# A residual stage that also prepares the next one, and filler products between the rotary stage and the compression

## The chip, the cores and the metric

The kernel runs on one core of a Trainium2 chip. The metric is the device time of one execution, in microseconds (us); lower is better.

## The reference

Two blocks of two layers each work on 512 tokens of width 1024; the second block has 256 context tokens beside them. Around each product stands a norm and a residual:

```python
def rms_norm(x, g):
    xf = x.astype(jnp.float32)
    y = xf * lax.rsqrt(jnp.mean(xf * xf, axis=-1, keepdims=True) + RMS_EPS)
    return (y * g.astype(jnp.float32)).astype(x.dtype)

def hybrid_layer(...):                       # first block, 2 layers
    hn = rms_norm(x, norm_g[0])
    ... = split_columns(hn @ w_in)           # queries, keys, values, gates
    kc = compress_blocks(k_c, cmp_pe[0], cmp_w1[0], cmp_w2[0])   # gelu(blocks @ w1) @ w2
    ks = partial_rope(k_s, positions)
    ...
    x = x + rms_norm(mixed, norm_g[1])
    hf = rms_norm(x, norm_g[2])
    ff = jnp.square(jax.nn.relu(hf @ w_ff1)) @ w_ff2
    return x + rms_norm(ff, norm_g[3])
```

The second block first computes `modulate(rms_norm_2(x, g), shift, scale)` over all 768 tokens and multiplies it by the latent attention's down projections; its second layer does the same ahead of a gated linear attention, whose first product is the small gate product. All is in float32; products that need the accuracy are made of three products of split operands (high and low parts).

## The kernel before

Features lie on the partitions: `x` is a tile of 128 partitions x 8 feature tiles (`KT`) x 768 tokens (512 and 256 of context). The program is a row of stages, each an `nc.Block()`, in which every engine has its own list of instructions; a stage begins when every engine has finished the one before. The two layers of the first block are one hardware loop (`nc.Fori(0, DEPTH)`).

Names that the change touches:

- `Norm`: ScalarE squares a feature tile (L237) into one of two buffers, TensorE adds it into PSUM with a product by a matrix of ones (L262); a square waits until the sum two tiles back is made. Then the root (L246, ScalarE), a turn to columns (L303, TensorE), the reciprocal and the diagonals (L316, L319, VectorE), and the spread back over the partitions (L309, TensorE). `keep_busy` issues products of constants that nothing reads (L205).
- `Normed`: VectorE scales (L355), ScalarE rounds to the high part (L368), VectorE subtracts for the low part (L346, L348); `first_tiles` multiplies feature tile by feature tile as the low parts come.
- `Residual`: VectorE scales `y` (L393); VectorE adds even tiles to `x` and GpSimd the odd ones (both L387).
- Weights come in units of 1 MB through two buffers `w_raw`; `load_unit` issues them on SyncE's queue, `split_hi` (ScalarE, L146) or `split_first` (VectorE, L411) rounds a unit, `split_lo` (VectorE, L152) subtracts.
- `sem_scope`: at its end, in a stage of its own, SyncE clears every semaphore made in it, one after the other (L2592). The layer loop's body is one scope, so this is done once in a layer, ahead of the branch (L2546).
- `stage_residual` holds nothing but a norm's spread and the residual. The stage behind it (`stage_qkv` at the head of a layer, `stage_modulation` and `stage_norm_dense` "down" at the head of the second block, `stage_norm_dense` "gate1" in its second layer) loads its small tables and two weight units, squares and sums `x`, and takes the root, then multiplies.
- `stage_rope`: TensorE permutes, VectorE and GpSimd rotate. `stage_compress`: VectorE adds positions to blocks (L604), TensorE multiplies them (L616, 64 instructions that are all queued behind each other).

Of the kernel before, what the change touches and what calls it, by code (L numbers as in the profile page):

```python
# [26 lines left out]
P = 128  # L27
# [180 lines left out]
class Norm:  # L208
# [10 lines left out]
    def __init__(self, k, name, src, kt, tok, bank, it=0, sems=None):  # L219
# [3 lines left out]
        self.name = name  # L223
# [20 lines left out]
    def act_root(self, act):  # L244
        act.wait_ge(self.summed, self.kt * (self.it + 1))
        act.activation(self.k.root[:, 0:self.tok], self.sums[0:1, :], ACT.Sqrt,  # L246
                       bias=self.k.c["eps"][0:1, 0:1]).then_inc(self.root, 1)
# [25 lines left out]
    def dve_gather(self, dve, t):  # L273
        k, tok = self.k, self.tok
        if t == 0:
            return
        acc = k.acc[:, 0:tok]
        dve.wait_ge(self.squared, t + 1)
        if t >= 2:
            dve.wait_ge(self.gathered, t - 1)  # L280
        dve.tensor_tensor(acc, k.sqt[:, 0, 0:tok] if t == 1 else acc, k.sqt[:, t % 2, 0:tok],
                          ALU.add).then_inc(self.gathered, 1)

# [148 lines left out]
def stage_qkv(nc, k, b, stream, first_unit):  # L432

    norm = Norm(k, "n1", k.x, KT, SEQ, 5)
# [4 lines left out]
    g_loaded = k.sem("g_loaded")  # L439

    with nc.Block() as block:
        @block.sync
        def _(sp):
            sp.dma_start(b.g, b.g_src).then_inc(g_loaded, 16)
            for n in range(n0, n0 + UNITS_QKV):
                load_unit(sp, k, n, stream(n))

        @block.tensor
        def _(pe):
            norm.pe_all(pe)  # L450
# [26 lines left out]
        @block.vector  # L477
        def _(dve):
            split_first(dve, k, n0)
            norm.dve_all(dve)  # L480
            dve.wait_ge(g_loaded, 16)
            normed.dve(dve)
            for u in range(2, UNITS_QKV):
                split_lo(dve, k, n0 + u)

        @block.scalar
        def _(act):
            norm.act_all(act)
# [39 lines left out]
def stage_rope(nc, k, b):  # L528
# [7 lines left out]
    with nc.Block() as block:  # L536
# [50 lines left out]
def stage_compress(nc, k, b):  # L587
# [8 lines left out]
    with nc.Block() as block:  # L596
# [13 lines left out]
        def _(pe):  # L610
# [16 lines left out]

            first_layer(0)
# [854 lines left out]
def stage_residual(nc, k, name, y, tok, post, y_norm=None):  # L1483

    norm = y_norm or Norm(k, f"{name}_p", y, KT, tok, 5)
    res = Residual(k, f"{name}_r", norm, k.x, post)
    with nc.Block() as block:  # L1487
        @block.tensor
        def _(pe):
            if y_norm is None:  # L1490
                norm.pe_all(pe)
            else:
                norm.pe_spread(pe)

        @block.scalar
        def _(act):
            if y_norm is None:
                norm.act_all(act)
            else:
                norm.act_root(act)  # L1500
# [11 lines left out]
def stage_rope_tables(nc, k, b, positions, inv_freq, inputs):  # L1512
# [8 lines left out]
    with nc.Block() as block:  # L1521
        @block.sync
        def _(sp):
            sp.dma_start(b.pos_i, positions.partition_broadcast(P)).then_inc(loaded, 16)
            sp.dma_start(b.inv, inv_freq).then_inc(loaded, 16)
            for dst, src in inputs:
                sp.dma_start(dst, src).then_inc(inputs_loaded, 16)
            sp.wait_ge(inputs_loaded, 16 * len(inputs))

        @block.vector  # L1530
        def _(dve):
# [23 lines left out]
            dve.sem_inc(sined, 1)  # L1555

# [8 lines left out]

# [9 lines left out]
def stage_modulation(nc, k, b, a, stream):  # L1575

    loaded, biased, scales = k.sem("mod_loaded"), k.sem("mod_biased"), k.sem("mod_scales")
    with nc.Block() as block:  # L1578
        @block.sync
        def _(sp):  # L1580
            for dst, src in ((b.ada_b, a["ada_b"]), (b.g, a["norm_g2"]), (b.axial, a["axial"]), (b.g_q, a["g_q"]),
                             (b.g_kv, a["g_kv"]), (b.g_o, a["g_o"])):
                sp.dma_start(dst, src).then_inc(loaded, 16)
            load_unit(sp, k, 0, stream(0))
            load_unit(sp, k, 1, stream(1))

        @block.vector
        def _(dve):
            dve.wait_ge(loaded, 96)
            dve.tensor_tensor(b.mod, b.mod, b.ada_b.unsqueeze(3).to_broadcast([P, ADA_TURNS, KT, 2]),  # L1590
                              ALU.add).then_inc(biased, 1)
            dve.wait_ge(biased, 1)
            for l in range(DEPTH):
                for j, (m, plus) in enumerate(((1, 1.0), (2, 0.0), (4, 1.0), (5, 0.0))):
                    g = b.g[:, l, j, :].unsqueeze(2).to_broadcast([P, KT, 2])
                    dve.scalar_tensor_tensor(b.sc[:, 4 * l + j, :, :], b.mod[:, 6 * l + m, :, :], plus, g, ALU.add,
                                             ALU.mult).then_inc(scales, 1)
            dve.wait_ge(scales, 4 * DEPTH)
# [12 lines left out]
def stage_norm_dense(nc, k, name, stream, n0, n_units, width, cols, out, tok, parts, after=2):  # L1611

    norm = Norm(k, f"{name}_n", k.x, KT, tok, 5)
# [3 lines left out]
    with nc.Block() as block:  # L1617
        @block.sync
        def _(sp):
            for n in range(n0 + 2, n0 + n_units + after):  # L1620
                load_unit(sp, k, n, stream(n))

        @block.tensor
        def _(pe):
            norm.pe_all(pe)
# [20 lines left out]
        def _(act):  # L1646
            norm.act_all(act)
# [721 lines left out]
def second_block(nc, k, a):  # L2369
# [3 lines left out]
    b = Bag()  # L2373
    stream = lambda n: a["stream2"][n]
    k.hhi, k.hlo = at("h_hi_2", [P, KT, TOK], F32R, 60), at("h_lo_2", [P, KT, TOK], F32R, 84)
    b.axial = at("axial", [P, TOK], F32, 108)
    b.mod = k.mod.rearrange("p (l t v) -> p l t v", t=KT, v=2)
    b.sc = at("norm_scales", [P, 4 * DEPTH, KT, 2], F32, 112.75)
    b.g_q, b.g_kv, b.g_o = at("g_q", [P, 3], F32, 113.25), at("g_kv", [P, 2], F32, 113.3125), at("g_o", [P, 2], F32, 113.375)
    b.st = at("mla_stat", [P, 8, 3], F32, 113.5)  # L2380
    b.ada_b, b.g = at("ada_b", [P, ADA_TURNS, KT], F32, 117), at("norm_g2", [P, DEPTH, 4, KT], F32, 118)
# [14 lines left out]
    rings(k, "second", 175)  # L2396
    mla_norm, mlp_norm = Norm(k, "mla_norm", y, KT, TOK, 1), Norm(k, "mlp0_norm", y, KT, TOK, 5)
    stage_modulation(nc, k, b, a, stream)
    n = 0

    with k.sem_scope():
        n = stage_norm_dense(nc, k, "down", stream, n, U_DOWN, UNIT, 256, down, TOK, parts_of(b, 0, 0, TOK, 0), 1)
# [6 lines left out]
    with k.sem_scope():  # L2409
        n = stage_mlp(nc, k, "mlp0", stream, n, y, hid_hi, hid_lo, TOK, parts_of(b, 0, 1, TOK), parts_of(b, 0, 2, TOK, 3), UNITS_2,  # L2410
                      mlp_norm, mla_norm)
        stage_residual(nc, k, "mlp0r", y, TOK, parts_of(b, 0, 3, TOK), mlp_norm)
# [13 lines left out]
                         parts_of(b, 1, 0, TOK, 0))  # L2426
# [16 lines left out]
def second_arrays(g, a):  # L2443
# [32 lines left out]
    a["stream2"] = np.concatenate(out)  # L2476
    assert a["stream2"].shape == (UNITS_2, P, UNIT)
# [10 lines left out]
def rings(k, sec, kb):  # L2488

    k.whi = k.at(f"w_hi_{sec}", [P, 2, UNIT], F32R, kb)  # L2490
    k.wlo = k.at(f"w_lo_{sec}", [P, 2, UNIT], F32R, kb + 16)


def first_block(nc, k, a):
# [6 lines left out]
    b.g, b.inv = at("norm_g1", [P, 4, KT], F32, 96), at("rope_inv", [P, 1], F32, 96.25)  # L2501
    b.pos_i = at("positions_i", [P, SEQ], I32, 97)
    stage_rope_tables(nc, k, b, a["positions"], a["inv_freq"],
                      [(k.x[:, :, 0:SEQ], a["x"]), (k.x[:, :, SEQ:TOK], a["ctx"]), (k.consts, a["consts"]), (k.cv, a["cvec"])])
# [41 lines left out]
    with nc.Fori(0, DEPTH) as layer, k.sem_scope(*k.w_loaded, k.w_hi, k.w_lo):  # L2546
        stream = lambda n: a["stream1"][layer, n]
        ada.layer, ada.src = layer, lambda n: a["ada_w"][layer, n]
        b.g_src = a["norm_g"][layer]
# [4 lines left out]
        n = stage_qkv(nc, k, b, stream, 0)  # L2554
# [7 lines left out]
        wo_norm, ff_norm = Norm(k, "wo_norm", y, KT, SEQ, 4), Norm(k, "ff_norm", y, KT, SEQ, 5)  # L2562
# [4 lines left out]
        stage_residual(nc, k, "ffr", y, SEQ, [(0, SEQ, b.g[:, 3, :])], ff_norm)  # L2567


def build(nc, a):  # L2570
    with ExitStack() as es:
# [9 lines left out]
        def sem_scope(*more):  # L2581
# [3 lines left out]
            with ExitStack() as stack:  # L2585
                k.scope = (stack, [])
                yield
                with nc.Block() as block:
                    @block.sync
                    def _(sp):  # L2590
                        for s in [*k.scope[1], *more]:
                            sp.sem_clear(s)  # L2592
                k.scope = outer

        k.sem, k.sem_scope = sem, sem_scope
# [8 lines left out]
        k.at = at  # L2604
# [11 lines left out]
        first_block(nc, k, a)  # L2616
        second_block(nc, k, a)
# [45 lines left out]
def host_arrays(i):  # L2663
# [8 lines left out]
    a["norm_g"] = np.ascontiguousarray(g["norm_g"].reshape(DEPTH, 4, KT, P).transpose(0, 3, 1, 2))  # L2672
# [3 lines left out]
    a["stream1"] = np.stack([stream_1(*(g[n][l] for n in ("w_in", "w_nsa_o", "w_sb_o", "w_out", "w_ff1", "w_ff2")))  # L2676
# [17 lines left out]
```

## Time and profile before

| | |
|---|---|
| time, median of 3 runs | 3806.79 us (3804.06 to 3808.51) |
| the profiled execution | 3811.21 us, of which the span from first to last instruction is 3809.4 us |
| TensorE products | 3497.2 us busy, 92% of the span |
| VectorE, ScalarE, GpSimd | 51%, 36%, 15% of the span |
| granted TensorE clock, mean | 0.961 of full |

The rows below are from that one profiled execution. A timeline row gives the start and the duration of a merged run of instructions in microseconds; in brackets stands the engine's idle time before it and what ended that. TensorE's clock is granted at one of two levels, 0.5 (1.2 GHz) and 1.0 (2.4 GHz); a value between them is a mean.

### The profile page before, as it was taken

The numbers are of one execution on the slowest core, as the hardware profiler recorded it, in microseconds if no ns is written. First come the engines' busy times: TensorE is split into PE (matmuls) and PEld (weight loads), VectorE is DVE, ScalarE is ACT, GpSimd is POOL, SyncE is SP. The second block draws the span as 40 slices with busy tenths as digits, with TensorE's granted clock in tenths as the row PEclk, the third lists the DMA queues.
The fourth block names the chain that finished last, engine by engine and source line by source line (L and its number), as shares of the span: only waits on it lengthen the run. The fifth ranks groups of instructions, "written<-read, shape, count | busy, mean of one in ns | idle before, by whom it ended". The sixth has DMA issues, their size and how long they took to land. (4 is left out here: it accounts for less than half of the span.)

```text
span 3809.4 us, 46818 instructions
## 1 busy us (share of the span) xinstructions
PE 3497.2 (92%) x17938; PEld 2880.7 (76%) x17938; DVE 1938.8 (51%) x2421; ACT 1354.8 (36%) x1976; POOL 552.5 (15%) x389
## 2 busy tenths in 40 slices
PE   8898999998889899999888989999999788889998
PEld 6675878887667687888667877888887677768886
DVE  4363347777337334777735652533334544455444
ACT  3275234443336523444323442221222423323222
POOL 0141003344024100433300110000000100010000
PEclk9999999999889899999999999999999899999999
DMA  3101224442210122444110011111111111102221
GB/s 134 69 1 56 99 100 155 154 155 76 101 58 1 66 88 100 155 162 158 67 50 23 18 36 48 56 57 65 66 59 41 44 35 44 44 33 89 96 91 66
DMA packets 58346, 287.18 MB, mean 75 GB/s; under 512 B 9824, under 2 KB 11104, under 8 KB 30944
## 3 DMA queue, kind: packets, MB, share of 16 engines
q1 hardware_dynamic: 58208, 285.34, 21.4%
q8 instruction: 87, 1.43, 0.2%
q14 instruction: 51, 0.42, 0.0%
HBM read 283.21 MB, written 2.10 MB: 75 GB/s over the span
## 5 line engine op out<-in xcount | busy, mean ns | idle before, releaser
L163 PE MATMUL ps<-h_hi,w_hi_rest 128*128 128x512 f32 (+1 forms) x1072 | 388.1, 362 | 27.4 <-DVE w_lo_rest L152 16.1
L164 PE MATMUL ps<-h_lo,w_hi_rest 128*128 128x512 f32 (+1 forms) x1072 | 366.9, 357 | 0.0
L1302 POOL TENSOR_TENSOR ada_context<-ada_context,ada_scaled 128x768 f32<-128x768 f32 x112 | 287.5, 2567 | 455.2 <-ACT ada_scaled L1384 450.1
L166 PE MATMUL ps<-h_hi,w_lo_rest 128*128 128x512 f32 (+1 forms) x1072 | 324.7, 358 | 0.0
L152 DVE TENSOR_TENSOR w_lo_mix<-w_raw,w_hi_mix 128x2048 fp32r<-128x2048 f32 x96 | 221.6, 2310 | 199.6 <-ACT w_hi_mix L146 199.5
L163 PE MATMUL ps<-h_hi,w_hi_mix 128*128 128x512 f32 x768 | 299.6, 390 | 4.6 <-DVE w_lo_mix L152 2.4
L164 PE MATMUL ps<-h_lo,w_hi_mix 128*128 128x512 f32 x768 | 299.1, 390 | 0.0
L166 PE MATMUL ps<-h_hi,w_lo_mix 128*128 128x512 f32 x768 | 299.1, 389 | 0.0
L387 POOL TENSOR_TENSOR x<-x,y 128x512 f32<-128x512 f32 (+1 forms) x32 | 63.8, 1994 | 1555.7 <-DVE y L393 1555.7
L146 ACT ACTIVATE w_hi_rest<-w_raw 128x2048 fp32r<-128x2048 f32 x82 | 156.3, 1908 | 360.1 <-PE ps L166 357.2
L1466 DVE TENSOR_TENSOR y<-ps,y 128x512 f32<-128x512 f32 (+1 forms) x224 | 165.8, 751 | 218.6 <-PE ps L166 217.9
L163 PE MATMUL ps<-hid_hi,w_hi_rest 128*128 128x512 f32 (+1 forms) x768 | 273.3, 356 | 0.0
L163 PEld LDWEIGHTS ps<-h_hi,w_hi_rest 128*128 128x128 f32 x1072 | 203.5, 190 | 80.6 <-DVE h_lo L348 14.3
L164 PE MATMUL ps<-hid_lo,w_hi_rest 128*128 128x512 f32 (+1 forms) x768 | 260.7, 354 | 0.0
L1397 ACT ACTIVATE sq<-ps 128x512 f32<-128x512 f32 (+1 forms) x128 | 83.4, 651 | 473.1 <-PE ps L166 473.1
L152 DVE TENSOR_TENSOR w_lo_rest<-w_raw,w_hi_rest 128x2048 fp32r<-128x2048 f32 (+1 forms) x85 | 195.9, 2307 | 70.3 <-ACT w_hi_rest L146 70.2
L166 PE MATMUL ps<-hid_hi,w_lo_rest 128*128 128x512 f32 (+1 forms) x768 | 231.2, 355 | 0.0
L146 ACT ACTIVATE w_hi_mix<-w_raw 128x2048 fp32r<-128x2048 f32 x94 | 178.9, 1905 | 145.2 <-PE ps L166 134.1
L164 PEld LDWEIGHTS ps<-h_lo,w_hi_rest 128*128 128x128 f32 x1072 | 203.7, 190 | 29.7
L1440 DVE SCALAR_TENSOR_TENSOR ada_latent<-ada_raw,cvec,ada_latent 128x768 f32<-128x768 f32 x112 | 225.4, 2012 | 0.0
L205 PE MATMUL ps<-consts 128*128 128x128 f32 x700 | 109.4, 313 | 112.6 <-PEq L1578 25.6
L163 PE MATMUL ps<-hid_hi,w_hi_mix 128*128 128x512 f32 x512 | 205.7, 402 | 0.1
(392 smaller groups left out, 7823.2 us busy)
## 6 DMA issues: line engine op xcount, KB each, us to landing
w_raw<-in_stream SPq DMA_DIRECT2D x205, 1024.0 KB, 4.8
ada_raw<-in_ada_w SPq DMA_DIRECT2D x128, 384.0 KB, 5.0
cmp_w<-in_cmp_w SPq DMA_DIRECT2D x8, 1024.0 KB, 7.3
mla_raw<-in_stream SPq DMA_DIRECT2D x8, 512.0 KB, 3.6
x<-in_x SPq DMA_DIRECT2D x1, 2048.0 KB, 8.6
out<-x SPq DMA_DIRECT2D x1, 2048.0 KB, 7.3
x<-in_ctx SPq DMA_DIRECT2D x1, 1024.0 KB, 10.8
consts<-in_consts SPq DMA_DIRECT2D x1, 832.0 KB, 12.0
```

The lines of the kernel that those rows point to most:

```text
L146: act.activation(k.whi[:, n % 2, 0:width], k.raw[:, n % 2, 0:width], ACT.Copy).then_inc(k.w_hi, 1)
L152: dve.tensor_tensor(k.wlo[:, n % 2, 0:width], k.raw[:, n % 2, 0:width], k.whi[:, n % 2, 0:width].bitcast(F32), ALU.subtract).then_inc(k.w_ ...
L163: pe.matmul(out, whi, xhi, start=start, stop=False)
L164: pe.matmul(out, whi, xlo, start=False, stop=False)
L166: last = pe.matmul(out, wlo, xhi, start=False, stop=stop)
L205: pe.matmul(k.ps[:, bank * 512:bank * 512 + P], k.c["ones"], k.c["ident"], start=True, stop=True)
L387: e.tensor_tensor(self.x[:, t, 0:n.tok], self.x[:, t, 0:n.tok], n.src[:, t, 0:n.tok], ALU.add).then_inc(sem, 1)
L1302: pool.tensor_tensor(ada.context, ada.context, ada.scaled[:, j % 2, :], ALU.add).then_inc(m["context"], 1)
L1397: act.activation(k.sqt[:, j % 2, 0:tok], k.ps[:, base:base + tok], ACT.Relu).then_inc(s["relu"], 1)
L1440: dve.scalar_tensor_tensor(ada.latent, ada.raw[j], k.cv[:, j, 0:1], ada.latent, ALU.mult, ALU.add).then_inc(m["latent"], 1)
L1466: dve.tensor_tensor(y[:, j, 0:tok], src, y[:, j, 0:tok], ALU.add).then_inc(s["added"], 1)
```

## The change

Four things are done.

1. `stage_residual` takes the next stage's norm with it. ScalarE squares each tile of `x` as soon as the residual has added it. At the end of a layer it also rounds the next stage's first two weight units. `x`'s norm there covers all 768 tokens, in every layer: first the eight context parts (256 columns each), then the eight parts of 512 columns, with 6 filler products between. The head of the kernel does the same in the stage of the rotary tables. The stages `qkv`, `down` and `gate1` no longer have a norm of their own.
2. SyncE issues, in the layer's last residual stage, the next layer's (or the second block's) first two weight units and seven small tables, and clears the semaphores of all stages behind it. For this it clears four semaphores of the weight ring first; ScalarE and VectorE wait for that (`reset`).
3. `stage_modulation` is gone; its nine VectorE instructions stand ahead of `normed.dve` in the stage "down". The weights of both blocks are one tensor in memory.
4. 16 products of constants at the end of TensorE's list in `stage_rope`, and 3 at the head of its list in `stage_compress`.

```diff
+    def pe_context_first(self, pe):
+        for t in range(self.kt):
+            self.pe_add_cols(pe, t, t, SEQ, CTX)
+        keep_busy(pe, self.k, 6, self.free)
+        for t in range(self.kt):
+            self.pe_add_cols(pe, self.kt + t, t, 0, SEQ)
+        self.pe_spread(pe)
+    def act_context_first(self, act, before=None):
+        for t in range(self.kt):
+            self.act_square_cols(act, t, t, SEQ, CTX)
+        for t in range(self.kt):
+            if before is not None:
+                before(act, t)
+            self.act_square_cols(act, self.kt + t, t, 0, SEQ)
+        self.act_root(act)
...
 def stage_qkv
-            sp.dma_start(b.g, b.g_src).then_inc(g_loaded, 16)
-            for n in range(n0, n0 + UNITS_QKV):
+            for n in range(n0 + 2, n0 + UNITS_QKV):
                 load_unit(sp, k, n, stream(n))
+            for sem in norm.sems:
+                sp.sem_clear(sem)
...
-            norm.pe_all(pe)
...
-            split_first(dve, k, n0)
-            norm.dve_all(dve)
-            dve.wait_ge(g_loaded, 16)
+            dve.tensor_copy(b.g, b.g_next).then_inc(g_taken, 1)
+            dve.wait_ge(g_taken, 1)
             normed.dve(dve)
...
 def stage_rope
+            pe.wait_ge(half2, 1)
+            keep_busy(pe, k, 16, 0)
...
 def stage_compress
+            keep_busy(pe, k, 3, 6)
             first_layer(0)
...
 def stage_residual
+            norm.pe_spread(pe)
+            if next_unit is not None:
+                next_norm.pe_context_first(pe)
+            elif next_norm is not None:
+                next_norm.pe_all(pe)
...
+            if reset is not None:
+                act.wait_ge(reset, 1)
+            norm.act_root(act)
+            if next_unit is not None:
+                next_norm.act_context_first(act, res.wait)
+                split_hi(act, k, next_unit + 1, (k.w_lo, next_unit + 1))
+            elif next_norm is not None:
+                next_norm.act_all(act, res.wait)
...
+            if reset is not None:
+                dve.wait_ge(reset, 1)
             norm.dve_all(dve)
             res.dve(dve)
+            if next_unit is not None:
+                res.wait(dve, KT - 2)
+                res.wait(dve, KT - 1)
+                split_first(dve, k, next_unit, 1)
+            if next_norm is not None:
+                next_norm.dve_all(dve)
+            if next_unit is not None:
+                split_lo(dve, k, next_unit + 1)
...
 def stage_rope_tables
+            for n in range(2):
+                load_unit(sp, k, n, stream(n))
             sp.wait_ge(inputs_loaded, 16 * len(inputs))
+        @block.tensor
+        def _(pe):
+            norm.pe_context_first(pe)
...
+            split_first(dve, k, 0)
+            norm.dve_all(dve)
...
             act.wait_ge(silu, 1)
-
+            norm.act_table(act)
+            norm.act_context_first(act)
...
 def stage_norm_dense
-            norm.pe_all(pe)
...
-            split_first(dve, k, n0, min(n_units, 2), width)
-            norm.dve_all(dve)
+            if before is not None:
+                before(dve)
+            if split < min(n_units, 2):
+                split_first(dve, k, n0 + split, min(n_units, 2) - split, width)
             normed.dve(dve)
...
 def first_block
+        finished = [sem for sem in k.scope[1] if sem not in ff_norm.sems]
+        reset = k.sem("ffr_reset")
+        def prefetch(sp):
+            for sem in (*k.w_loaded, k.w_hi, k.w_lo):
+                sp.sem_clear(sem)
+            sp.sem_inc(reset, 1)
+            for i in range(2):
+                load_unit(sp, k, i, a["stream"][(layer + 1) * UNITS_1 + i])
...
+            for dst, src in loads:
+                sp.dma_start(dst, src).then_inc(small_loaded, 16)
+            k.clear(sp, finished)
+            sp.wait_ge(small_loaded, 16 * len(loads))
+            sp.sem_clear(small_loaded)
```

## Rows read from the trace of the kernel before

**Rows 1.** The page, part 1: busy us (share of the span) and instructions
```profile
PE 3497.2 (92%) x17938; PEld 2880.7 (76%) x17938; DVE 1938.8 (51%) x2421; ACT 1354.8 (36%) x1976; POOL 552.5 (15%) x389
```

**Rows 2.** Timeline, end of layer 0 (start, duration, engine, line, operation, count, idle before)
```profile
936.07 0.68 ACT L246 ACTIVATE acc<-ps,consts 1x512 f32<-1x512 f32 x1 [2.21 <-PEq L1272]
939.99 1.41 DVE L393 SCALAR_TENSOR_TENSOR y<-y,norm_g,ps 128x512 f32<-128x512 f32 x2 [0.67 <-PE ps L309]
947.23 1.64 POOL L387 TENSOR_TENSOR x<-x,y 128x512 f32<-128x512 f32 x1 [0.27 <-DVE y L393]
```

**Rows 3.** Line L2592, clears, 949 to 958 us; then 2959 to 2961 us
```profile
L2592 SPq EVENT_SEMAPHORE_RANGE_CLEAR  x134: 25/30/49, 949.2 to 957.2; - x134
...
L2592 SPq EVENT_SEMAPHORE_RANGE_CLEAR  x23: 25/25/30, 2959.4 to 2960.6; - x23
```

**Rows 4.** Line L2546, the layer loop's branch (duration ns min/median/max, starts)
```profile
L2546 PEldq COMPARE_BRANCH  x2: 83/1728/3372, 957.7 to 1907.9; - x2
```

**Rows 5.** Timeline, layer 1's first norm
```profile
966.64 0.63 ACT L237 ACTIVATE sq<-x 128x512 f32<-128x512 f32 x1 [0.60 <-PE ps L262]
970.33 0.63 ACT L237 ACTIVATE sq<-x 128x512 f32<-128x512 f32 x1 [0.36 <-PE ps L262]
971.83 4.49 DVE L152 TENSOR_TENSOR w_lo_qkv<-w_raw,w_hi_qkv 128x2048 fp32r<-128x2048 f32 x2
971.98 1.05 PE L205 MATMUL ps<-consts 128*128 128x128 f32 x8
976.24 0.18 DVE L316 RECIPROCAL norm_stat<-ps 128x4 f32<-128x4 f32 x1
978.90 1.41 DVE L355 SCALAR_TENSOR_TENSOR sq<-x,norm_g,ps 128x512 f32<-128x512 f32 x2 [1.58 <-PE ps L309]
```

**Rows 6.** Timeline, start of the kernel
```profile
18.92 0.63 ACT L237 ACTIVATE sq<-x 128x512 f32<-128x512 f32 x1
29.28 0.68 ACT L246 ACTIVATE acc<-ps,consts 1x512 f32<-1x512 f32 x1 [1.22 <-PE ps L262]
33.05 1.41 DVE L355 SCALAR_TENSOR_TENSOR sq<-x,norm_g,ps 128x512 f32<-128x512 f32 x2 [0.67 <-PE ps L309]
```

**Rows 7.** Timeline, layer 1 to the second block
```profile
1897.47 1.64 POOL L387 TENSOR_TENSOR x<-x,y 128x512 f32<-128x512 f32 x1 [0.27 <-DVE y L393]
1907.92 0.35 SPq L1583 DMA_DIRECT2D ada_b<-in_ada_b  x1
1914.45 0.77 DVE L1596 SCALAR_TENSOR_TENSOR norm_scales<-mod,norm_g 128x16 f32<-128x16 f32 x8
1935.02 2.19 DVE L355 SCALAR_TENSOR_TENSOR sq<-x,norm_scales,ps 128x512 f32<-128x512 f32 x4 [0.72 <-PE ps L309]
```

**Rows 8.** Timeline, second residual to the gate product
```profile
2956.61 2.45 POOL L387 TENSOR_TENSOR x<-x,y 128x768 f32<-128x768 f32 x1 [0.50 <-DVE y L393]
2961.69 1.23 DVE L152 TENSOR_TENSOR w_lo_rest<-w_raw,w_hi_rest 128x1024 fp32r<-128x1024 f32 x1
2979.87 2.19 DVE L355 SCALAR_TENSOR_TENSOR sq<-x,norm_scales,ps 128x512 f32<-128x512 f32 x4 [0.72 <-PE ps L309]
```

**Rows 9.** Timeline, the MLP stage that already has residual and norm in one block
```profile
2379.78 3.59 POOL L387 TENSOR_TENSOR x<-x,y 128x768 f32<-128x768 f32 x1 [0.49 <-DVE y L393]
2390.59 2.19 DVE L355 SCALAR_TENSOR_TENSOR sq<-x,norm_scales,ps 128x512 f32<-128x512 f32 x4 [0.72 <-PE ps L309]
```

**Rows 10.** Timeline, rotary stage and compression of layer 0
```profile
152.21 0.42 PE L557 MATMUL ps<-consts,gate_t 24*128 24x24 f32 x4
159.59 16.04 PE L616 MATMUL ps<-cmp_w,blk 128*31 128x256 f32 x64 [6.96 <-DVE blk L604]
```

**Rows 11.** Windows there and in layer 1 (us, busy time and count of each engine, clock, DMA share, GB/s)
```profile
156.00:157.00 1.00, 0.00 (x0) 0.00 (x0) 0.97 (x2) 0.00 (x0) 0.57 (x1) 0.96 1.02 426
163.00:164.00 1.00, 1.00 (x4) 0.45 (x3) 0.00 (x0) 0.00 (x0) 0.00 (x0) 0.62 0.00 0
...
1106.00:1110.00 4.00, 3.81 (x11) 1.71 (x12) 1.57 (x4) 0.81 (x1) 0.00 (x0) 0.59 0.01 6
```

More of the change, by code:

```diff
@@ L244, in act_root @@
     def act_root(self, act):
-        act.wait_ge(self.summed, self.kt * (self.it + 1))
+        act.wait_ge(self.summed, self.adds * (self.it + 1))
         act.activation(self.k.root[:, 0:self.tok], self.sums[0:1, :], ACT.Sqrt,
@@ L282, in dve_gather, with act_square_cols, pe_add_cols @@
                           ALU.add).then_inc(self.gathered, 1)
+    def act_square_cols(self, act, i, t, c0, w):
+        k = self.k
+        if i >= 2:
+            act.wait_ge(self.summed, i - 1)
+        act.activation(k.sqt[:, i % 2, c0:c0 + w], self.src[:, t, c0:c0 + w], ACT.Square,
+                       scale=float((self.kt * P) ** -0.5)).then_inc(self.squared, 1)
+    def pe_add_cols(self, pe, i, t, c0, w):
+        k = self.k
+        pe.wait_ge(self.squared, i + 1)
+        pe.matmul(self.sums[:, c0:c0 + w], k.c["ones"], k.sqt[:, i % 2, c0:c0 + w],
+                  start=t == 0, stop=t == self.kt - 1).then_inc(self.summed, 1)
+    def act_context_first(self, act, before=None):
[13 more added lines that the diff above has]
+        self.pe_spread(pe)
     def pe_sum(self, pe):
@@ L1509, in _, with stage_rope_tables @@
             res.pool(pool)
-def stage_rope_tables(nc, k, b, positions, inv_freq, inputs):
+def stage_rope_tables(nc, k, b, positions, inv_freq, inputs, norm, stream):
     loaded, chain, sined = k.sem("rt_loaded"), k.sem("rt_chain"), k.sem("rt_sin")
@@ L1572, with modulation @@
 MLA_SCALE = float(192 ** -0.5)
[L1575 to L1598, printed above, removed]
+def modulation(dve, k, b):
+    biased, scales = k.sem("mod_biased"), k.sem("mod_scales")
+    dve.tensor_tensor(b.mod, b.mod, b.ada_b.unsqueeze(3).to_broadcast([P, ADA_TURNS, KT, 2]),
+                      ALU.add).then_inc(biased, 1)
+    dve.wait_ge(biased, 1)
+    for l in range(DEPTH):
+        for j, (m, plus) in enumerate(((1, 1.0), (2, 0.0), (4, 1.0), (5, 0.0))):
+            g = b.g[:, l, j, :].unsqueeze(2).to_broadcast([P, KT, 2])
+            dve.scalar_tensor_tensor(b.sc[:, 4 * l + j, :, :], b.mod[:, 6 * l + m, :, :], plus, g, ALU.add,
+                                     ALU.mult).then_inc(scales, 1)
+    dve.wait_ge(scales, 4 * DEPTH)
 def parts_of(b, layer, norm, tok, shift=None):
@@ L1608, in parts_of, with stage_norm_dense @@
     return out
-def stage_norm_dense(nc, k, name, stream, n0, n_units, width, cols, out, tok, parts, after=2):
-    norm = Norm(k, f"{name}_n", k.x, KT, tok, 5)
+def stage_norm_dense(nc, k, name, stream, n0, n_units, width, cols, out, tok, parts, norm, split=0, after=2, before=None):
     normed = Normed(k, f"{name}_h", norm, k.hhi, k.hlo, parts)
@@ L1621, in _ @@
                 load_unit(sp, k, n, stream(n))
+            for sem in norm.sems:
+                sp.sem_clear(sem)
         @block.tensor
         def _(pe):
-            norm.pe_all(pe)
             unit_ready(pe, k, n0)
@@ L2394, in second_block @@
     hid_hi, hid_lo = at("hid_hi2", [P, 4, TOK], F32R, 127), at("hid_lo2", [P, 4, TOK], F32R, 139)
-    rings(k, "second", 175)
-    mla_norm, mlp_norm = Norm(k, "mla_norm", y, KT, TOK, 1), Norm(k, "mlp0_norm", y, KT, TOK, 5)
-    stage_modulation(nc, k, b, a, stream)
+    rings(k, "qkv", 175)
+    mla_norm, mlp_norm = Norm(k, "mla_norm", y, KT, TOK, 1), Norm(k, "mlp0_norm", y, KT, TOK, 1)
+    gate_norm = Norm(k, "gate_norm", k.x, KT, TOK, 5)
     n = 0
     with k.sem_scope():
-        n = stage_norm_dense(nc, k, "down", stream, n, U_DOWN, UNIT, 256, down, TOK, parts_of(b, 0, 0, TOK, 0), 1)
+        n = stage_norm_dense(nc, k, "down", stream, n, U_DOWN, UNIT, 256, down, TOK, parts_of(b, 0, 0, TOK, 0), k.x_norm, 2, 1,
+                             lambda dve: modulation(dve, k, b))
         stage_norm(nc, k, "cq", down[:, 0:3, :], 3, b.cq_hi, b.cq_lo, b.g_q)
@@ L2501, in first_block @@
     b.g, b.inv = at("norm_g1", [P, 4, KT], F32, 96), at("rope_inv", [P, 1], F32, 96.25)
+    b.g_next = at("norm_g_next", [P, 4, KT], F32, 96.5)
+    k.x_norm = Norm(k, "x_norm", k.x, KT, TOK, 5, adds=2 * KT)
+    small_loaded = k.sem("small_loaded")
+    rings(k, "qkv", 175)
+    second = Bag()
+    second_tables(k, second)
     b.pos_i = at("positions_i", [P, SEQ], I32, 97)
     stage_rope_tables(nc, k, b, a["positions"], a["inv_freq"],
-                      [(k.x[:, :, 0:SEQ], a["x"]), (k.x[:, :, SEQ:TOK], a["ctx"]), (k.consts, a["consts"]), (k.cv, a["cvec"])])
+                      [(k.x[:, :, 0:SEQ], a["x"]), (k.x[:, :, SEQ:TOK], a["ctx"]), (k.consts, a["consts"]), (k.cv, a["cvec"]), (b.g_next, a["norm_g"][0])],
+                      k.x_norm, lambda n: a["stream"][n])
     b.sbq, b.sbk, b.sbv = at("sbq", [P, 4, SEQ], F32, 97), at("sbk", [P, 4, SEQ], F32, 105), at("sbv", [P, QT, 512], F32, 113)
@@ L2591, in _, with clear @@
                         for s in [*k.scope[1], *more]:
-                            sp.sem_clear(s)
+                            if s not in cleared:
+                                sp.sem_clear(s)
                 k.scope = outer
+        cleared = []
+        def clear(sp, sems):
+            for s in sems:
+                sp.sem_clear(s)
+            cleared.extend(sems)
+        k.clear = clear
         k.sem, k.sem_scope = sem, sem_scope
```

79 lines of the change are left out of this document (40 added, 39 removed).

## The prediction

> **What bounds the kernel now.** The page's engine shares come first [rows 1]: TensorE is busy for 92% of the span, so the kernel is a chain of products and the time that can go is the time in which TensorE does not do a real product. VectorE and ScalarE are half idle or more. The chain of waits is of little use here (it follows back only a few steps), so I read the timeline around each place that the diff touches. In it the reader is to see four stretches with no real product: the head of the kernel up to 33 us [rows 6], the turn from layer 0 to layer 1 [rows 2, 5], the turn into the second block [rows 7] and the way from the second block's first residual to the gate product [rows 8]. Then I asked the windows for TensorE's clock where filler products are added [rows 11].
>
> **The turn from layer 0 to layer 1, before.** GpSimd adds the last tile of x until 947.23 + 1.64 = 948.87 us [rows 2]. 134 clears run from 949.2 to 957.2, one each 0.060 us [rows 3]. The branch of the loop holds TensorE's sequencer from 957.7 for 3.37 us [rows 4]. Then the norm squares, sums, and its result is first used at 978.90 [rows 5]: 30.0 us behind the residual.
>
> **The same, after.** (a) ScalarE and VectorE wait for `reset`, behind four clears: 4 x 0.06 plus signalling, 0.35 us. Behind that wait stand the root, and so the whole residual. The spread ends and y is scaled at 939.99 + 0.35 = 940.3. (b) TensorE is then free and adds the eight context parts. Their squares are ScalarE's, which waits for nothing but the two buffers. No row shows this step. The full parts repeat every (970.33 - 966.64) / 4 = 0.92 us [rows 5]. A 256-column float32 product is two instructions; 64 such instructions took 16.04 us with some 4 us at the lower clock level [rows 10, 11], so about 0.21 each and 0.43 a product. The step lies between 0.43 and 0.92; I take 0.6, as half the columns leave the signals between the engines as they are: 8 x 0.6 = 4.8, to 945.1. (c) Six filler products, 1.05 / 4 = 0.26 each [rows 5]: 1.6, to 946.7. (d) Eight full parts: 0.85 for one whose square lies ready, and seven steps of 0.92: 7.3, to 954.0. The last tile of x is there at 949.2, so the sums and not the residual now end last. (e) From the root to the scaled result the kernel's head shows 33.05 - 29.28 = 3.77 with VectorE free [rows 6]: 957.8. (f) One `split_lo` of 4.49 / 2 = 2.25 stands behind it on VectorE [rows 5], 960.1, and the whole stage ends with it. The other copy and subtraction (1.2 + 2.25, from 949.2) lie under the sums; if they were late they would delay the columns, and they are done at 952.7 against a need at about 956. (g) A barrier of 0.3, 12 clears that are left (the norm's 8, the residual's 3, reset) 0.7, to 961.1; the way from the last clear to the top of the loop stays 961.07 - 957.2 = 3.9 [rows 3, 4], 965.0; the copy of the small table 0.3: 965.3. Gain 978.9 - 965.3 = 13.6. (h) TensorE has now been idle from 957.8 to the top of the loop. After 152.63, its last product in the rotary stage [rows 10], the clock fell at about 156.96 [rows 11], so I expect it low at the first tiles, for some 2 us more than before: minus 1.0. Net gain 12.6.
>
> On this point a page bears. The Trainium skill ("Runtime: NRT & Kernel Launch", Instruction fetch mechanics) says that a taken branch to code outside the fetched window stalls for the fetch. The row of the branch agrees, 3.37 us when it is taken and 0.08 when it is not. By that rule the saving in clears would still stand, and only the turn itself is beyond this change.
>
> SyncE's own list in that stage must not be the last to end: 4 clears, two loads and seven tables at some 0.5 each, 111 clears at 0.06: 0.24 + 4.5 + 6.7 = 11.4 us from 936.1, 947.5, against 960.1. Twelve microseconds are to spare, and the weights, issued at 936.5, have 12 us to land before their copy. Where that cover is gone, each microsecond costs one.
>
> **The turn into the second block.** The same stage runs 1897.47 - 947.23 = 950.24 us later [rows 2, 7]: the norm is ready at 957.8 + 950.24 = 1908.0, the stage ends at 1910.3, barrier and 12 clears to 1911.3, 0.4 to the next block (as 1907.5 to 1907.92 before), the nine VectorE instructions of the modulation, 0.77 for the eight small ones [rows 7] and, as an estimate, as much again for the one of 192 columns and the two waits, 1.4: 1913.1 instead of 1935.02, 21.9. Gone are the 122 clears, the wait for tables, the norm over 768 tokens. Minus 1.0 for the clock again: 20.9.
>
> **The gate product.** The MLP stage already has residual and norm of this shape in one block: its last tile of x is ready at 2379.78 + 3.59 = 2383.37 and the norm is used at 2390.59, 7.2 us later [rows 9]. Here the last tile is ready at 2956.61 + 2.45 = 2959.06 [rows 8]: norm at 2966.3. Then the 23 clears, as before [rows 3], 1.9 from end to next stage: 2968.2. `split_first` of the 512 KB unit, which lay under the norm, now stands bare ahead of the scaling: 1.23 for the subtraction [rows 8] and some 0.7 for the copy, 1.9. 2970.1 against 2979.87: 9.8.
>
> **The head of the kernel.** This part is slower. The first square stays at 18.9 us (its table load is behind the same `silu`) [rows 6], but eight context parts, whose sums nobody uses in layer 0, and six fillers now stand ahead of the full ones. Eight parts are 4.8 at the rate above, some at the lower clock level, at which a product takes 0.85; the fillers are 1.6; against it, the full parts no longer start cold, and before they lost about 2. 5.4 as the sum, with 0.6 for a stage border. The earlier weights gain nothing: the splits ended before the columns were asked for, within 0.3 us.
>
> **The filler products.** Compression starts at 159.59 [rows 10]; the clock is at 0.62 in the microsecond from 163.0, that is low up to 163.76 [rows 11]: 4.2 us at half speed, half of it lost, 2.1. In layer 1 the 4 us from 1106 have 0.59, low for 3.1 us of work: 1.5. The 16 products are 4.2 us long from 152.6, all inside the 6.96 us in which TensorE waited for VectorE's rotation and its first addition of positions [rows 10]; the three others lie there too, behind the border of the stages. Gain 3.6 if the clock stays up; bounds 0 and 3.6.
>
> The Trainium skill ("TensorE: Matmul & The Clock Gate", HAM oscillation) has it that gaps without products put the clock down and that the next stretch pays. The trace agrees with the direction: it fell after 4.3 us of idleness. By that page the fillers would pay, and the idle turns (h) would cost, which is the same sum.
>
> **Small.** The second block's first scope clears 8 semaphores fewer: 0.5 gained.
>
> **The sum.** 12.6 + 20.9 + 9.8 + 3.6 + 0.5 - 5.4 = 42.0 us gained. The profiled execution took 3811.2, so it would take 3769.2; the median shown is 4.4 under the profiled one: 3764.8, say 3765.
>
> **The rivals.**
> 1. *TensorE is cold in the new sums.* The context parts use TensorE for 0.43 of 0.6 us; if that is too little to hold the clock, the full parts take up to 1.7 instead of 0.92, about 6 us for each of the two turns and 2 at the head. For it: the clock is down after this very stage before. Against it: TensorE was idle then, and now it works from 940.3 on. Gain 42 - 14 = 28: 3779.
> 2. *Code arrives late.* Straight-on stage borders had no fetch in sight, because the clears gave 8 us for it. If each border of the three behind the new stages costs what the branch costs, 3.4, the turn into the second block and the gate product lose 6.8: 3772. Against it: the border from norm to MLP stages shows no such gap.
> 3. *SyncE ends last.* Issues of 2 us instead of 0.5 use up the 12 us: 0 to 3 us a turn, 3765 to 3771.
> 4. *The other side: the clock stays low behind the turns.* At each of the three turns the first tiles now meet an idle TensorE. If they, paced by VectorE, do not bring the clock back, the products of `qkv`, 111 us at full level, double. It decides from 84 us of added low level on (half of it lost makes 42); every low stretch that the rows show ended within 6 us of work. Time 3850 and more.
> 5. *Nothing happens:* the clears are hidden behind the branch's fetch. The rows exclude it: the branch starts behind the last clear.
> 6. *The sums are faster than I think:* context steps at 0.43 and the clock up through the turns, 2 x (1.4 + 1.0) + 1.4 + some signals, 8 more: 3757.
>
> **How the numbers follow.** The forecast as summed, with terms 2 to 3 us off either way, has 0.55; rival 1 0.17, rival 2 0.10, rival 3 0.04, rival 6 0.11, rival 4 with everything else that makes it slower 0.02, and 0.01 for no change. The range goes from rival 6 with a few microseconds to rival 1: 3752 to 3781. A measurement of this kernel can tell 0.2%, 7.6 us, from no change; all cases but the last are beyond it: faster 0.97, same 0.01, slower 0.02.
>
> **What the changed profile would show.** Some 111 clears beside the residual's work and 12 behind it; first scaling in layer 1 some 13.6 us nearer to the last root of layer 0, and 21.9 nearer at the second block; a later first scaling at the head, 38.5 instead of 33.05; 64 compression instructions in about 13.9 us at clock 1.00; the scaling for the gate product 11 us behind the last tile of x. Wrong would make it: a clock of 0.5 between the context parts and the root, VectorE waiting for columns long after 956, or an engine's list that starts late behind a border.

## The result, and the profile after

The changed kernel took 3778.19 us (median of 4 runs, 3769.97 to 3779.29) against 3806.71 before: 0.9921 of the time, with an interval of 0.9904 to 0.9938. The forecast was 3765, in a range of 3752 to 3781. So the direction was right, and of 42 us that were forecast 28.5 came. The same kernel measured a second time took 3770.49 (5 runs, 3769.98 to 3775.00), ratio 0.9904 (0.9890 to 0.9918): part of the answer is already in that difference. The rows below are from the first profile of the changed kernel (3778.84 us, span 3777.1) unless another is named.

The turn from layer 0 to layer 1 in the changed kernel, timeline, engine by engine (answers to [rows 2, 5]):

```profile
946.27 0.68 ACT L246 ACTIVATE acc<-ps,consts 1x512 f32<-1x512 f32 x1 [2.42 <-SPq L2625]
949.85 4.65 PE L294 MATMUL ps<-sq,consts 128*128 128x256 f32 x16
950.05 1.41 DVE L423 SCALAR_TENSOR_TENSOR y<-y,norm_g,ps 128x512 f32<-128x512 f32 x2 [0.66 <-PE ps L339]
...
955.67 7.61 PE L294 MATMUL ps<-sq,consts 128*128 128x512 f32 x16
957.29 1.65 POOL L417 TENSOR_TENSOR x<-x,y 128x512 f32<-128x512 f32 x1 [0.27 <-DVE y L423]
...
963.31 0.89 ACT L246 ACTIVATE acc<-ps,consts 1x768 f32<-1x768 f32 x1 [1.22 <-PE ps L294]
968.00 2.29 DVE L152 TENSOR_TENSOR w_lo_qkv<-w_raw,w_hi_qkv 128x2048 fp32r<-128x2048 f32 x1 [0.72 <-PE ps L339]
975.17 0.18 DVE L508 COPY norm_g<-norm_g_next 128x32 f32<-128x32 f32 x1 [4.88 <-issue]
975.39 1.41 DVE L385 SCALAR_TENSOR_TENSOR sq<-x,norm_g,ps 128x512 f32<-128x512 f32 x2
```

The whole turn lies 10.06 us later than before (957.29 against 947.23), which is itself a finding. Less that, it is close to the forecast: the last tile of x at 958.94, the root 4.4 us behind it because the sums end last (the 512-column products until 963.28), the stage's end with the last subtraction at 970.29, the first scaling at 975.39 - 10.06 = 965.33. The forecast was 965.3; the gain is 13.6.

The clears in it, by line (answers to [rows 3]), and the branch [rows 4]:

```profile
L2680 SPq EVENT_SEMAPHORE_RANGE_CLEAR  x111: 25/30/49, 951.6 to 958.3; - x111
...
L2673 SPq EVENT_SEMAPHORE_RANGE_CLEAR  x12: 25/28/30, 970.6 to 971.2; - x12
...
L2599 PEldq COMPARE_BRANCH  x2: 83/1865/3647, 971.7 to 1910.4; - x2
```

111 of the clears lie beside the residual and the sums. The taken branch still holds TensorE's sequencer, now for 3.65 us.

The head, the turn into the second block and the gate product, timeline (answers to [rows 6 to 8]):

```profile
33.39 0.89 ACT L246 ACTIVATE acc<-ps,consts 1x768 f32<-1x768 f32 x1 [1.22 <-PE ps L294]
38.89 1.41 DVE L385 SCALAR_TENSOR_TENSOR sq<-x,norm_g,ps 128x512 f32<-128x512 f32 x2
...
1895.99 1.65 POOL L417 TENSOR_TENSOR x<-x,y 128x512 f32<-128x512 f32 x1 [0.26 <-DVE y L423]
1911.62 1.80 DVE L385 SCALAR_TENSOR_TENSOR sq<-x,norm_scales,ps 128x512 f32<-128x512 f32 x3
...
2931.36 2.47 POOL L417 TENSOR_TENSOR x<-x,y 128x768 f32<-128x768 f32 x1 [0.50 <-DVE y L423]
2937.83 0.89 ACT L246 ACTIVATE acc<-ps,consts 1x768 f32<-1x768 f32 x1 [1.68 <-PE ps L262]
2940.88 1.60 PE L339 MATMUL ps<-diag,consts 128*128 128x128 f32 x12
2944.58 0.69 DVE L441 CAST w_hi_rest<-w_raw 128x1024 fp32r<-128x1024 f32 x1 [2.77 <-PEq L2668]
2946.45 2.18 DVE L385 SCALAR_TENSOR_TENSOR sq<-x,norm_scales,ps 128x512 f32<-128x512 f32 x4
```

The head is 5.84 us later than before (5.4 forecast). From the last tile's start to the first scaling at the second block are 15.63 us, 37.55 before: 21.9 gained, as forecast. At the gate product they are 15.09 instead of 23.26: 8.2, where 9.8 were forecast.

### The profile page after: what moved, and what is told of

Its sections match the earlier page's. It is cut to its first block and busy times, and to the rows that moved or that the text cites. A ratio compares the mean times of both kernels' runs of the same rounds, so it can differ in the third digit from the quotient of the medians.

```text
span 3777.1 us, 47197 instructions
## 1 busy us (share of the span) xinstructions
PE 3519.8 (93%) x18068; PEld 2895.0 (77%) x18068; DVE 1936.7 (51%) x2425; ACT 1363.8 (36%) x1997; POOL 553.6 (15%) x389
## 5 line engine op out<-in xcount | busy, mean ns | idle before, releaser
L164 PE MATMUL ps<-hid_lo,w_hi_mix 128*128 128x512 f32 x512 | 200.6, 392 | 0.0
```

The lines of the kernel that those rows point to most:

```text
L164: pe.matmul(out, whi, xlo, start=False, stop=False)
```

## The experiments

The ratio is to the kernel before, measured beside the kernel of the row. Kernels of different rows were not all measured beside each other, so ratios are compared and not medians.

| kernel | median us | ratio (95% interval) |
|---|---|---|
| changed, first time | 3778.19 | 0.9921 (0.9904 to 0.9938) |
| changed, again | 3770.49 | 0.9904 (0.9890 to 0.9918) |
| before + fillers only | 3808.67 | 1.0003 (0.9994 to 1.0012) |
| changed, no fillers in rotary stage and compression | 3771.05 | 0.9898 (0.9883 to 0.9913) |
| changed, norm of 512 columns at the head | 3768.50 | 0.9894 (0.9879 to 0.9909) |
| changed, no fillers between the parts | 3770.89 | 0.9896 (0.9881 to 0.9912) |
| changed, 10 / 20 tiny activations at the head | 3774.72 / 3775.77 | 0.9912 / 0.9919 (0.9898 to 0.9927 / 0.9905 to 0.9933) |
| the three omissions together (fillers of rotary stage and compression, 512 columns at the head, no fillers between the parts) | 3766.88 | 0.9892 (0.9876 to 0.9908) |
| changed, all clears at the end | 3791.41 | 0.9952 (0.9938 to 0.9965) |
| changed, 26 fillers in the rotary stage | 3779.03 | 0.9916 (0.9902 to 0.9929) |
| three omissions + late subtraction | 3762.56 | 0.9878 (0.9863 to 0.9893) |
| that + fillers at the turns | 3767.52 | 0.9890 (0.9875 to 0.9905) |

**The filler products.** Without them, alone on the old kernel, and with more of them:

```diff
-            pe.wait_ge(half2, 1)
-            keep_busy(pe, k, 16, 0)      # or 26
...
-            keep_busy(pe, k, 3, 6)
```

> The kernel before with only the filler products (16 in the rotary stage, 3 in the compression). Theory A (the fillers hold the clock, the prediction's term): 3.6 us faster, about 3803, and the 64 compression instructions take 13.9 us in both layers. Theory B (the clock falls in the 2.5 us that stay without a product behind the fillers, depending on where that gap lies in time): between 0 and 2 us faster, and in at least one layer the compression still starts at the lower level. In either, what lies behind the compression is only shifted; if theory B holds more widely, the low stretches elsewhere (348, 940 us) may come or go with the shift.

> The changed kernel without the filler products. Theory A: 3.6 us slower than the changed one, 3782. Theory B: within 3 us of the changed kernel on either side, since the fillers gained 0.4 us in layer 0 and 1.3 in layer 1 there and the rest is where the clock happens to fall.

> The changed kernel with 26 instead of 16 fillers at the end of the rotary stage, so that TensorE has no gap of 2.6 us ahead of the compression. Theory A (a filled wait keeps the clock): the compression's 64 instructions take 13.9 us in both layers, and what the 16 fillers gained or not becomes 3.5 us against the kernel without fillers in the profile up to the compression; the whole is within the spread of 3770 to 3779. If the clock still falls at the compression's head, the fall is not tied to the gap.

The compression in layer 0 and in layer 1, one pair for each kernel: the changed one, the same again, 26 fillers, fillers alone on the old kernel, and changed without fillers (timeline, TensorE; 14.00 us is what it took where the granted clock stayed at 1.00, and the old kernel took 16.04 and 15.49):

```profile
165.75 15.55 PE L645 MATMUL ps<-cmp_w,blk 128*31 128x256 f32 x64
1106.16 14.00 PE L645 MATMUL ps<-cmp_w,blk 128*31 128x256 f32 x64
```
```profile
166.13 14.00 PE L645 MATMUL ps<-cmp_w,blk 128*31 128x256 f32 x64
1101.44 15.69 PE L645 MATMUL ps<-cmp_w,blk 128*31 128x256 f32 x64
```
```profile
165.76 14.00 PE L645 MATMUL ps<-cmp_w,blk 128*31 128x256 f32 x64
1109.48 14.00 PE L645 MATMUL ps<-cmp_w,blk 128*31 128x256 f32 x64
```
```profile
159.59 14.00 PE L618 MATMUL ps<-cmp_w,blk 128*31 128x256 f32 x64
1108.13 14.91 PE L618 MATMUL ps<-cmp_w,blk 128*31 128x256 f32 x64
```
```profile
165.67 16.09 PE L643 MATMUL ps<-cmp_w,blk 128*31 128x256 f32 x64 [6.96 <-DVE blk L631]
1100.33 16.38 PE L643 MATMUL ps<-cmp_w,blk 128*31 128x256 f32 x64 [6.96 <-DVE blk L631]
```

With 16 fillers a gap of about 2.6 us is left ahead of the last three, and in one layer or the other the clock falls all the same. With 26 it held in both layers, 4.5 us less in the two products than without any. And yet that kernel is not faster than the one without fillers (0.9916 against 0.9898), and fillers alone make 1.0003. What the compression gains was not there at the end.

In layer 0 it is already gone in the next products, those of the queries with the compressed keys. Without fillers, then with 26:

```profile
183.97 4.32 PE L702 MATMUL ps<-kc,q 64*128 64x31 f32 x64 [0.55 <-PEq L623]
181.97 6.18 PE L705 MATMUL ps<-kc,q 64*128 64x31 f32 x64 [0.54 <-PEq L625]
```

They start 2.0 us earlier with the fillers and end 0.14 us earlier: from 184 to 188 us the granted clock is 0.87 without and 0.50 with fillers. The changed kernel's second profile shows the same (start 182.34, end 187.93). It is not so in every case: in the old kernel with fillers alone 1.5 of 2.0 us are still there behind these products, and 2.5 us go at about 930, where its granted clock is 0.57 from 928 to 936 and the old kernel's is 1.00. In the profile of 26 fillers the clock is low for 10 us at the end of layer 0's MLP stage, where the changed kernel's second profile shows no low stretch.

**Where the time goes that the terms don't have.** The changed kernel unedited, and with a short delay at its head:

```diff
             norm.act_table(act)
+            for i in range(10):          # or 20
+                act.activation(k.diag[:, i:i + 1], k.c["ones"][:, 0:1], ACT.Sqrt)
             norm.act_context_first(act)
```

> The changed kernel itself, unedited, beside the runs of this call. Both theories: its ratio to the kernel before again about 0.992 (3778). If the clock's falls are tied to nothing in the program, single executions spread by up to 9 us, as 3770 and 3779 did, and the profile shows other low stretches than the first profile of the changed kernel.

> The changed kernel with ten ScalarE activations of one column ahead of the context squares at the head: everything behind starts some 1.5 to 2 us later and nothing else changes. Theory A (the terms add up): 2 us slower than the changed kernel, with a constant shift over the whole trace. Theory B (where the clock falls depends on where a thin stretch lies in time): the shift starts at +2 us and then jumps by 1 to 3 us at the ends of the MLP stages (937, 1876), at the turns and at the compression; the median lies up to 8 us to either side of the changed kernel.

> As the run with ten, with twenty activations: 3 to 4 us later at the head. Theory A: 4 us slower than the changed kernel. Theory B: anywhere between 5 us faster and 10 us slower, with other low stretches than with ten.

Windows of 14 us over the end of layer 0's MLP stage, in which no code was changed (us, busy time and count of PE, PEld, DVE, ACT, POOL, granted clock, DMA): the changed kernel, the same again, then with 10 and with 20 activations:

```profile
930.00:944.00 14.00, 13.49 (x63) 11.64 (x62) 9.62 (x14) 3.77 (x7) 1.87 (x1) 0.76 0.00 0
```
```profile
930.00:944.00 14.00, 12.22 (x74) 9.85 (x72) 9.22 (x13) 4.90 (x10) 0.95 (x1) 1.00 0.01 2
```
```profile
930.00:944.00 14.00, 12.22 (x72) 9.85 (x71) 9.85 (x13) 4.27 (x8) 1.59 (x1) 1.00 0.00 1
```
```profile
930.00:944.00 14.00, 12.56 (x70) 10.02 (x68) 10.89 (x14) 3.77 (x7) 2.55 (x2) 1.00 0.00 0
```

And the last root of layer 0, as a landmark just behind it, in the same four kernels:

```profile
946.27 0.68 ACT L246 ACTIVATE acc<-ps,consts 1x512 f32<-1x512 f32 x1 [2.42 <-SPq L2625]
```
```profile
942.87 0.68 ACT L246 ACTIVATE acc<-ps,consts 1x512 f32<-1x512 f32 x1 [2.42 <-SPq L2625]
```
```profile
943.50 0.68 ACT L246 ACTIVATE acc<-ps,consts 1x512 f32<-1x512 f32 x1 [2.42 <-SPq L2627]
```
```profile
944.53 0.68 ACT L246 ACTIVATE acc<-ps,consts 1x512 f32<-1x512 f32 x1 [2.42 <-SPq L2627]
```

The same code, executed again, is 3.4 us earlier there, and its span is 3768.2 instead of 3777.1. Most of that arises in one place: between the starts of the same two VectorE instructions lie 2.46 us in the second profile (936.56 to 939.02) and 4.95 in the first (937.48 to 942.43), while VectorE waits for TensorE. Just ahead of it TensorE has one-column products (L1351) between those of 512 columns, in both profiles, and is as busy in both (3.49 of 4 us from 933 in the first, 3.48 from 932.1 in the second). In the first the clock falls at 937, in the second it does not. At the end of layer 1's MLP stage the first profile loses another 2.5 us in the same way (granted clock 0.81 from 1868 to 1886, 1.00 in the second from 1861 to 1879). The kernels whose first scaling is 1.2 and 2.3 us later at the head are still earlier at the root than the first. And the old kernel with fillers alone, in which nothing of the turn was changed, has a low stretch there too. So the fall of the clock in this stretch belongs to no line of the change, and it comes and goes between executions of one program.

Theory A (a constant shift) is out: against the second profile, the kernel with ten activations is 0.8 us later at the head and 4.1 at the end. Theory B is not shown: the delays don't prove that the place is set by time in the program, since the unedited kernel moves as much by itself. The medians of both, 4.2 and 5.3 us above the unedited kernel measured beside them, have intervals that overlap with its own.

**The head and the six fillers.**

```diff
-                      k.x_norm, lambda n: a["stream"][n])
+                      Norm(k, "x_norm", k.x, KT, SEQ, 5, 0, k.x_norm.sems), lambda n: a["stream"][n])
...
-            norm.pe_context_first(pe)
+            norm.pe_all(pe, 0)
...
-            norm.act_context_first(act)
+            norm.act_all(act)
```
```diff
-        keep_busy(pe, self.k, 6, self.free)      # in pe_context_first
```

> The changed kernel, but at the head of the kernel the norm squares and sums only the 512 columns that layer 0 reads (no context part, no six fillers, no fillers ahead of the sums). The sum of the prediction: 5.8 us faster than the changed kernel, with the first scaling at 33 instead of 38.9 us: 3772. The rival (the clock's falls move with the shift): the first scaling is as early, but the median lies anywhere from 3766 to 3778, by which of the stretches at 348, 937 and 976 us run at the lower level.

> The changed kernel without the six filler products between the context parts and the full parts of the norm's sums. The sum of the prediction: 1.5 us at each of three places, 4.5 us faster: 3774. The rival: the full parts start at the lower level without them, and nothing is gained or up to 3 us lost at a place.

> The changed kernel with all three edits: a norm of 512 columns at the head, no six fillers between the parts, no fillers in the rotary stage and the compression. Theory A: 5.8 + 3.0 faster from the first two, 3.6 slower from the third: 3773. Theory B (fillers are worth about nothing here): 5.8 + 3.0 faster and up to 5 us from where the clock falls: 3765, between 3761 and 3770.

The first scaling with 512 columns, timeline:

```profile
27.20 0.68 ACT L246 ACTIVATE acc<-ps,consts 1x512 f32<-1x512 f32 x1 [1.22 <-PE ps L262]
31.64 1.41 DVE L385 SCALAR_TENSOR_TENSOR sq<-x,norm_g,ps 128x512 f32<-128x512 f32 x2
```

It is 7.3 us earlier than in the changed kernel and 1.4 earlier than in the kernel before: all that the head lost comes from the context part and its six fillers; layer 0 doesn't read the context's norm. The medians fit a gain, but the intervals of 0.9894 and 0.9896 overlap with both of the changed kernel's; each alone isn't settled. The three together, 0.9892, are no better than one of them. At the turn the six fillers cost less than I counted: from root to root 17.04 us with them (946.27 to 963.31) and 16.32 in the kernel where they alone are gone (943.58 to 959.90), 0.7 and not 1.6. Without them TensorE waits 0.35 us for ScalarE's square at the first of the full parts, so they lie in part in a wait.

**The early clears.** One line is taken out; the scope then clears all 123 at its end:

```diff
-            k.clear(sp, finished)
```

> The changed kernel with the early clears undone: the 111 semaphores are cleared at the end of the layer's scope again, with the 12 others. The sum of the prediction: 111 x 0.06 = 6.7 us on the path at each of the two turns, 13.3 us slower than the changed kernel in the same call of runs, that is 3784 to 3792, and 123 clears between the end of the residual stage and the branch. A rival: the clears lie beside something else (the branch's fetch of code) and cost less, under 8 us in all.

```profile
L2672 SPq EVENT_SEMAPHORE_RANGE_CLEAR  x123: 25/30/49, 969.3 to 976.8; - x123
...
962.03 0.89 ACT L246 ACTIVATE acc<-ps,consts 1x768 f32<-1x768 f32 x1 [1.22 <-PE ps L294]
981.22 1.41 DVE L385 SCALAR_TENSOR_TENSOR sq<-x,norm_g,ps 128x512 f32<-128x512 f32 x2
```

From the root to the first scaling 19.19 us, against 12.08 in the changed kernel: 7.1 for one turn, 6.7 expected. As a whole its ratio is 0.0048 above the changed kernel's second one, which makes 18 us, and 0.0031 above the first, 12 us; two turns of 7.1 are between them. The rival of hidden clears is out.

**The last subtraction moved as well.** With the three omissions, and the second unit's low part moved behind the turn. The main lines are shown; the stage "down" subtracts it in the same way, and at the head of the kernel it leaves `split_first`:

```diff
-            if next_unit is not None:
-                split_lo(dve, k, next_unit + 1)
...
             normed.dve(dve)
-            for u in range(2, UNITS_QKV):
+            for u in range(1, UNITS_QKV):
```

And in a second kernel, on top of it, fillers:

```diff
                 next_norm.pe_context_first(pe)
+                keep_busy(pe, k, 10, 3)
...
-    keep_busy(pe, k, 3 * (tok // 256) - 1)      # in first_tiles
+    keep_busy(pe, k, 3 * (tok // 256) + 4)
```

> The kernel with all three edits, and also the low part of weight unit 1 is subtracted in the stage behind the turn, behind the scaled parts, not ahead of the turn. The prediction's term (f) says 2.25 us off the path at each of two turns; the subtraction now ends behind the first tiles and TensorE may wait for it up to 1.5 us each. 1.5 to 4.5 us faster than with the three edits: 3763 to 3765.

> As the run before, with ten fillers behind the spread in the layer's residual stage and five more ahead of the first tiles of each stage. Theory B: the low stretch at the first tiles behind the turns (3.3 us lost in the first profile of the changed kernel, 1.4 at the second block) gets shorter where the fillers leave no gap over 5 us: 0 to 4 us faster than without them. Against it: fillers ahead of first tiles that are ready cost 1.3 us each where TensorE is the later one.

From root to first scaling (timeline), and the end of TensorE's list in the residual stage with the fillers:

```profile
955.14 0.89 ACT L246 ACTIVATE acc<-ps,consts 1x768 f32<-1x768 f32 x1 [1.22 <-PE ps L294]
965.14 1.41 DVE L384 SCALAR_TENSOR_TENSOR sq<-x,norm_g,ps 128x512 f32<-128x512 f32 x2
```
```profile
956.34 0.89 ACT L246 ACTIVATE acc<-ps,consts 1x768 f32<-1x768 f32 x1 [1.22 <-PE ps L294]
959.38 1.60 PE L338 MATMUL ps<-diag,consts 128*128 128x128 f32 x12
960.83 2.40 PE L205 MATMUL ps<-consts 128*128 128x128 f32 x20
968.37 1.41 DVE L384 SCALAR_TENSOR_TENSOR sq<-x,norm_g,ps 128x512 f32<-128x512 f32 x2
```

10.00 us, 2.1 less than in the changed kernel, as term (f) says. 3762.56 is the lowest median of all kernels here; the interval of its ratio lies below that of the changed kernel's first measurement and overlaps with that of the second and with that of the three omissions, so as a gain of the whole kernel the subtraction's move isn't settled. Fillers at the turns were expected to gain 0 to 4 us, and the median is 5 us higher (the intervals of the ratios overlap). Their ten products stand behind the spread (over at 960.98) and end at 963.23, so now the stage ends with them: from root to first scaling they make it 12.03 us, and 2.0 of the 2.1 are lost again.

## Why the prediction was right, and where it was off

The measured 3778.19 lies in the range because the range reached up to rival 1 (3779), and rival 1 is not what happened: the mechanism of the turns was right, the number of the sum was 13.4 us too low, and that the result stands beside rival 1's number is chance.

- *The turn's steps (a) to (g):* right, 13.6 and 21.9 us, by experiment for the clears (7.1) and for the last subtraction (2.1). The context parts took 4.65 us for eight, 4.8 forecast. Two errors inside cancel, which is luck: the fillers of step (c) cost 0.7 instead of 1.6, and step (e), root to result, took 4.7 (963.31 to 968.00) instead of 3.77. The norm now has 768 tokens, and the row that I took it from had 512. The old trace had the right one, 4.69 us from the root below to 2979.87 [rows 8]:

```profile
2975.18 0.89 ACT L246 ACTIVATE acc<-ps,consts 1x768 f32<-1x768 f32 x1 [1.74 <-PE ps L262]
```

- *Rival 1* (TensorE cold in the new sums) did not occur at the turns: the granted clock is 1.00 from 946 to 968 us, and from 1896 to 1908 in layer 1.
- *Rivals 2, 3 and 5* (late code, SyncE last, hidden clears) did not occur. The second block's first scaling came at the forecast distance, 15.63 us, and at the gate product 2.1 us lie between the spread's end (2942.48) and the next stage's first instruction, clears included, where the sum had 1.9. SyncE's clears ended at 958.3, twelve us ahead of the stage's end.
- *The head:* 5.8 lost, 5.4 forecast.
- *The gate product:* 9.8 was 8.2. The last tile's distance to the result came from a stage in which it is 7.2, with the root 2.5 us behind the tile; here the root starts 4.0 us behind it, the sums being late.
- *Step (h):* 1.0 a turn was mis-sized. In the first profile the way from first scaling to the next weight unit grew by 3.3 us in layer 1 and 1.4 at the second block, the clock staying low until 985. In the second profile it grew by 2.1 and 0.5. This is rival 4's mechanism in small.
- *The filler products:* the term of 3.6 is what failed as a gain of the kernel. Locally it exists (0.5 + 1.5 in the first profile, 4.5 with 26 fillers against none), at the end of the kernel it was not measurable. The prediction counted a low stretch removed as time gained, and left out that the clock can fall in the next products instead, as it did in layer 0, and that such stretches come and go elsewhere.
- *What the sum lacked:* a term for stretches without changed code. The first profile lost 1.5 us near 347 and 2.5 near 937 there; the second has neither.
- *The first profile, added up:* its span is 32.3 us under the old one's, 9.7 less than the sum. The gate product is 1.6 of that, the head 0.4, step (h) 2.7, the fillers 1.6 and the two unchanged stretches 4.0, together 10.3. The rest of the 13.4 is the subtraction of 4.4 us from profile to median, which the old kernel's profiled execution gave: the changed kernel's was only 0.65 above its median.
- *The second profile* has a span of 3768.2, 41.2 under the old one's, where 42.0 had been forecast. That is luck in part: the gate product's error is in it too, and a low stretch of the old kernel behind 2058 us, worth 1.5 us and in unchanged code, is missing in it. That the two profiles of one kernel differ by 8.9 us, in the main where one has a low stretch and the other has not, is what the runs show. What places the falls stays open.

## What to carry to other kernels

Clearing and loading for the next stage beside the present stage's work paid in full here, where the queue that does it had twelve us of slack, and the chain of steps at the turn could be summed from rows of the old trace to within a microsecond; take each row from a place with the same shape. Don't count on a filler product's local gain: look at the products right behind it, and measure the whole kernel, several times and on more than one occasion. A filler at the end of a stage's list can itself become what the stage ends with. Where a stage is shared by a loop's turns, look for what only the last turn needs; at the head the context part made the first scaling 5.8 us later and was of no use to layer 0.

## What I had not expected of the hardware

The same program's executions differ by 9 us (3769.97 and 3779.29). Two that were profiled, at 3778.84 and 3769.98, put this in the main on the clock level granted to TensorE in a few stretches: 0.76 or 1.00 from 930 to 944 us, in the same part of the program. Behind the same gap of 2.6 us without products, three fillers later, the granted clock fell in the first profile of the changed kernel (0.51 from 166 to 169 us), and in its second profile it did not (1.00 from 162 to 170). And a fall that is kept off in one place can come right behind it: with 26 fillers the compression ran at 1.00 and the products from 184 to 188 us at 0.50.
